# Turning the cross-attention query columns inside the projection, and regrouping the projection's columns

## The chip, the cores and the metric

The kernel runs on one core of a Trainium2 chip, as one program on its five engines: TensorE (PE) multiplies, VectorE (DVE), ScalarE (ACT) and GpSimd (POOL) work on what it leaves in PSUM, and SyncE (SP) starts most of the transfers. The metric is the device time of one execution in microseconds; several executions are timed and their median stands.

## The reference

All tensors are fp32 and there are 256 tokens of width 1024. A first block (pooling mixer, MoBA attention, gated feed-forward) is followed by two layers of a second block. Each of these two layers projects its input, mixes tokens, attends to a memory of 256 rows, projects out, normalises, and runs a mixture of 16 experts. The change touches only how the two input projections are made:

```python
def second_block(x, mem, ...):
    for i in range(DEPTH_2):                       # two layers
        if kind == 0:                              # layer 1: NSA, w_in is 1024 x 2596
            proj = x @ nsa_w_in[j]
            mix = nsa_mixer(proj[..., :-XA_WIDTH], ...)
        elif kind == 1:                            # layer 2: MLA, w_in is 1024 x 672
            proj = x @ mla_w_in[j]
            mix = mla_mixer(proj[..., :-XA_WIDTH], mla_q_norm[j], mla_w_uq[j], ...)
        xq = proj[..., -XA_WIDTH:].reshape(B, S, XA_HEADS, HEAD_DIM_2)   # XA_WIDTH = 256: 4 heads of 64
        xa = memory_cross_attention(xq, mk, mv).reshape(B, S, XA_WIDTH)
        y = jnp.concatenate([mix, xa], -1) @ w_out[i]
        x = layer_norm(DEEPNORM_ALPHA * x + y, ...)
        f = hier_moe(x, ...)                       # 16 experts, each 3 x 1024 x 512
        x = layer_norm(DEEPNORM_ALPHA * x + f, ...)

def mla_mixer(mix_cols, q_norm, w_uq, kv_norm, w_ukv, cos_m, sin_m):
    c_q    = mix_cols[..., :256]                   # the latent vectors
    c_kv   = mix_cols[..., 256:384]
    k_rope = mix_cols[..., 384:416]
    q  = (rms_norm_2(c_q, q_norm) @ w_uq)...       # needs the whole row of c_q
    kv = (rms_norm_2(c_kv, kv_norm) @ w_ukv)...
```

## The kernel before

**The split product.** A large projection is an fp32 product made of three fp32r products (`three`, L796): both operands are split into a rounded high part and the rest, and high x high, high x low, low x high are added in PSUM. The activations lie turned (feature by token) as the pair `h1 = (hTr, yTr)`. Weights come by units of up to 512 columns (`by_cols`, L383) in three slots, and each unit is cut into four pieces of 256 weight rows. For each piece ACT writes the high part `phi` (`cast`, L1960, the copy at L1969) and DVE the low part `plo` (`cut`, L1344, the subtraction at L1349). There are four piece buffers, so a piece is cast when TensorE has used the piece four before it (`s_pc`); hence ACT and DVE cast and cut the *next* unit while TensorE multiplies the present one.

**Two forms of the product.** `tok3` (L818, steps at L805) keeps the activations stationary and moves the weights: two banks, one for each half of the tokens, hold token rows. `feat3` (L821) keeps 128x128 blocks of the weights stationary and moves the 256 tokens: the result comes turned, feature by token. Both record their matmuls at L798. A result in token rows that is wanted turned goes out of PSUM to SBUF and through TensorE's transposes (`turn_cols`, L749, recorded at L755), and out again.

**Layer 1 (the n stage, L992 to L1071).** Columns of `nsa_w_in` come as units n1, n2, n0, then n4 (2048 to 2560), n3 (1536 to 2048) and n5 (2560 to 2596, 36 columns). TensorE interleaves them with the compression of the keys (L1018), the turning of queries, and the compressed scores (`cs`, L1054, 30 columns wide). After n5 (L1057) it turns the window keys (`kw`) and the cross-attention queries (`xq`, L1062), then waits for `s_pcn` and turns the compressed probabilities (`pt`, L1068). `s_pcn` comes from DVE: a softmax over 15 compressed keys, whose first half (L1672 to L1680) goes to ACT for the exponentials (L2158) and whose second half (L1688 to L1700) stands in DVE's program behind `second_row(11, 5, 36, ...)` (L1682), the copy of n5's second result bank. The attention of this layer follows.

**Layer 2 (the m stage, L1258 to L1315).** Columns of `mla_w_in` come as m0 (0 to 512) and m1 (512 to 672, 160 columns), both by `tok3`; `pm` receives the token rows. DVE and ACT copy m1's banks behind the cutting and casting of the next unit's four pieces (ob0, L1873 to L1876 and L2252 to L2255). Only then come the norms' squares (ACT, L2262, four in a row), the variances (DVE, L1879), the inverse roots (POOL, L2307), the scaling (DVE, L1884), and the rotation of `k_rope` (DVE, L1888). TensorE waits for the copies, turns the cross-attention queries (L1266, L755), waits for the scaled latents, turns them (`cq`, `ck`, L1270), and after DVE's copies (L1892, L1895) runs six small projections (L1285, L1288) with the turning of heads between them (L1304). Banks are given in turn of four, so a head's transposes wait for the copy of the ones before (L1333).

**After each attention.** `out_proj`, a layer norm and the router run, then the experts: 96 halves of expert weights of 1 MB each go through 18 places (`expert_loads`, L677). SP issues them in order and waits before each for the event that frees its place: the first ones for the projections' last pieces and for the end of the attention (`s_pv`, 48 and 80), half 18 and on for TensorE's use of the half 18 before. The loads of ob1 and of the next layer's units stand in the same queue.

Of the kernel before, what the change touches and what calls it, by code (L numbers as in the profile page):

```python
# [15 lines left out]
KC = 8  # L16
# [142 lines left out]
def build(nc, ins, out, const, onehot, scratch):  # L159
    ctx = ExitStack()  # L160
    with ctx:
# [221 lines left out]
        def by_cols(name, w, n0, n):  # L383
            unit(name, [cols(w, KC, n0, n)], 2 * n, KC // 2)
# [33 lines left out]
        for c in (4, 3):  # L418
            by_cols(f"n{c}", w_n, c * 512, 512)
        unit("n5", [cols(w_n, KC, 2560, 36)], KC * 36, 1)  # L420
        by_cols("oa0", w_o2[0], 0, 512)
        by_cols("oa1", w_o2[0], 512, 512)
        by_cols("m0", w_m, 0, 512)
        by_cols("m1", w_m, 512, 160)
# [78 lines left out]
        B.work("n", 12, own=False)  # L503
# [17 lines left out]
        B.work("m", 4, own=False)  # L521
        for stage, n in (("xq2", 1), ("cq", 1), ("ck", 1)):
            B.work(stage, n)
# [205 lines left out]
        def tensor_program(e):  # L729
# [301 lines left out]
            tok3_steps(bks, h1, 512, p0, range(3))  # L1031
# [4 lines left out]
            tok3_steps(bks, h1, 512, p0, range(3, 4))  # L1036
# [20 lines left out]
            tok3_steps(two_banks("n", 10), h1, 36, first_piece("n5"), range(1), KC)  # L1057
            e.wait_ge(s_rope, 6)
            turn_cols("kw", pj, 1792 - 64, 5, 64)
            for i in range(10, 12):  # L1060
                e.wait_ge(*B.empty("n", i))
            turn_cols("xq", pj, 2340, 2)  # L1062
# [7 lines left out]
            await_empty("ks", "kw", "xq", "cc1")  # L1070
# [192 lines left out]
            tok3("m", 0, h1, 512, first_piece("m0"))  # L1263
            tok3("m", 2, h1, 160, first_piece("m1"))
            await_empty("m")
            turn_cols("xq2", pm, 416, 2)  # L1266
# [55 lines left out]
        def vector_program(e):  # L1322
# [323 lines left out]
            second_row(7, 4, 512, p0 + 3)  # L1646
# [35 lines left out]
            second_row(11, 5, 36, first_piece("n5"))  # L1682
# [190 lines left out]
            for n, (c0, w) in enumerate(((0, 512), (512, 160))):  # L1873
                p0 = first_piece(f"m{n}")
                cut(p0 + 4, p0 + 8)
                evac("m", 2 * n + 1, pm[:, 1, c0:c0 + w], B.ap("m", 2 * n + 1)[:, 0:w], None, used(p0 + 3, 1))  # L1876
# [18 lines left out]
            evac("ck", 0, ckT[:, 0, :], B.ap("ck", 0)[:, 0:256], colv[:, KN:KN + 1])  # L1895

# [20 lines left out]
            for n in range(6):  # L1917
                project(n)
                if n >= 2:
                    turned_heads(n - 2)  # L1920
# [7 lines left out]
        def scalar_program(e):  # L1928
# [215 lines left out]
            first_row(6, 4, 512, p0 + 3)  # L2144
# [14 lines left out]
            first_row(10, 5, 36, first_piece("n5"))  # L2159
            keys("kw", kwT)  # L2160
            evac("xq", 0, xqT, B.ap("xq", 0)[:, :].rearrange("p (c t) -> p c t", c=2), -0.125)
# [90 lines left out]
            for n, (c0, w) in enumerate(((0, 512), (512, 160))):  # L2252
                p0 = first_piece(f"m{n}")
                cast(p0 + 4, p0 + 8)
                evac("m", 2 * n, pm[:, 0, c0:c0 + w], B.ap("m", 2 * n)[:, 0:w], None, used(p0 + 3, 0))  # L2255
# [7 lines left out]
            evac("xq2", 0, xqT2, B.ap("xq2", 0)[:, :].rearrange("p (c t) -> p c t", c=2), -0.125)  # L2263
# [21 lines left out]
            for n in range(6):  # L2285
                project(n)
                if n >= 2:
                    turned_heads(n - 2)
# [9 lines left out]
        def pool_program(e):  # L2298
# [207 lines left out]
```

## Time and profile before

| | |
|---|---|
| median of 3 executions | 1183.96 us (1181.03 to 1193.82) |
| profiled execution, device time | 1182.21 us |
| its span, first to last instruction | 1180.1 us |
| mean granted TensorE clock (1.00 is 2.4 GHz) | 0.964 |
| PE busy | 1060.3 us, 90% of the span |
| DVE, ACT, POOL busy | 39%, 32%, 10% |
| HBM read | 294.58 MB, 251 GB/s over the span |

Every instruction has a start and a duration; a busy share says only that records cover the time. The steps between the starts of consecutive matmuls, not their own durations, give their price, since they overlap. The chain of waits is followed back from the last instruction and names what each step waited for.

### The profile page before, as it was taken

To read this page: it belongs to the slowest core of one execution; us is meant where nothing else is said; L and a number is where in the kernel's file an instruction comes from. 1 tells how busy PE (TensorE), PEld (TensorE's weight loads), DVE (VectorE), ACT (ScalarE), POOL (GpSimd) and SP (SyncE) were. 2 spreads that over 40 slices of the span, in tenths; PEclk is the share of its full clock that TensorE was granted. 3 is DMA by queue.
4 is the path that set the end of the run, shared out by engine and by line. 5 is a ranking of instruction groups with operands and counts; after the bars stand their busy time and mean duration, and the time that the engine had idled before them with its cause. 6 is when DMAs were issued, how large, how long until landed. Compare 5 with 4: busy or idle time off the path is not lost.

```text
span 1180.1 us, 15606 instructions
## 1 busy us (share of the span) xinstructions
PE 1060.3 (90%) x6167; PEld 730.3 (62%) x6167; DVE 457.6 (39%) x975; ACT 373.3 (32%) x726; POOL 121.8 (10%) x151
## 2 busy tenths in 40 slices
PE   5999999999998998997999999857888799999983
PEld 5967899998867787674644444326557464445431
DVE  4644566665466445654111111035555311111103
ACT  4443355554355454731111111114462111111101
POOL 0711011110001001420000000010042000000001
PEclk9999999999999998998899999988899889999998
DMA  9834665554454441079899999983319789999993
GB/s 338 189 142 137 218 208 174 185 192 165 159 198 145 141 175 46 2 282 346 325 387 386 386 387 387 387 312 110 126 46 337 278 326 387 386 386 387 387 388 124
DMA packets 164577, 296.95 MB, mean 252 GB/s; under 512 B 10975, under 2 KB 40847, under 8 KB 164495
## 3 DMA queue, kind: packets, MB, share of 16 engines
q1 hardware_dynamic: 162910, 290.08, 69.1%
q0 software_dynamic: 1584, 5.77, 1.3%
q8 instruction: 53, 0.87, 0.3%
q14 instruction: 30, 0.24, 0.1%
HBM read 294.58 MB, written 1.25 MB: 251 GB/s over the span
## 4 chain that ended last, share of the span: by engine, by line
PE 75%; DMA 8%; DVE 7%; ACT 5%; issue 3%; POOL 1%; POOLq 1%; DVEq 0%; SPq 0%; ACTq 0%
PE ps L798 32%; PE ps L1135 16%; PE ps L1149 6%; PE ps L1121 6%; DMA arena<-in_moe_w_down 3%; DMA arena<-in_moe_w_up 2%; DMA gain_rows<-in_moe_w_up 2%; PE ps L1162 2%; PE ps L900 2%; PE ps L869 1%; PE ps L879 1%; PE ps L792 1%; ACT ring L1998 1%; PE ps L1285 1%; POOL small L2307 1%
## 5 line engine op out<-in xcount | busy, mean ns | idle before, releaser
L1349 DVE TENSOR_TENSOR plo<-w,phi 128x1024 fp32r<-128x1024 f32 (+1 forms) x143 | 174.5, 1233 | 163.0 <-ACT phi L1969 162.5
L1969 ACT CAST phi<-w 128x1024 fp32r<-128x1024 f32 (+1 forms) x143 | 144.9, 1029 | 169.5 <-PE ps L798 161.1
L1135 PE MATMUL ps<-w,arena 128*64 128x512 f32 x528 | 135.7, 594 | 3.5 <-DMA w<-in_moe_w_up 3.5
L798 PE MATMUL ps<-hTr,phi 128*128 128x256 f32 x448 | 128.5, 287 | 4.5 <-DVE yTr L1339 4.5
L798 PE MATMUL ps<-hTr,plo 128*128 128x256 f32 x448 | 128.1, 286 | 0.0
L798 PE MATMUL ps<-yTr,phi 128*128 128x256 f32 x448 | 128.0, 286 | 0.0
L1829 DVE SCALAR_TENSOR_TENSOR yTr<-ps,small,yTr 128x512 fp32r<-128x512 f32 x32 | 24.0, 751 | 237.5 <-ACT yTr L2208 237.5
L798 PE MATMUL ps<-phi,hTr 128*128 128x512 f32 (+2 forms) x272 | 103.8, 382 | 6.3 <-DVE yTr L1339 6.3
L798 PE MATMUL ps<-phi,yTr 128*128 128x512 f32 (+2 forms) x272 | 103.5, 381 | 3.4 <-issue 1.9
L1149 PE MATMUL ps<-w,ring 128*64 128x512 f32 x336 | 92.4, 593 | 6.6 <-DMA w<-in_moe_w_down 3.6
L798 PEld LDWEIGHTS ps<-hTr,phi 128*128 128x128 f32 x448 | 87.4, 195 | 5.1 <-issue 3.1
L798 PEld LDWEIGHTS ps<-yTr,phi 128*128 128x128 f32 x448 | 87.4, 195 | 0.0
L798 PEld LDWEIGHTS ps<-hTr,plo 128*128 128x128 f32 x448 | 87.2, 195 | 0.0
L1135 PEld LDWEIGHTS ps<-w,arena 128*64 128x64 f32 x528 | 42.0, 137 | 72.7 <-issue 72.5
L1135 PE MATMUL ps<-arena 128*64 128x512 f32 x304 | 79.1, 594 | 4.4 <-DMA arena<-in_moe_w_up 4.4
L1121 PEld LDWEIGHTS ps<-mkT,x 128*128 128x128 f32 x512 | 67.8, 217 | 13.7 <-issue 9.7
L1121 PE MATMUL ps<-mkT,x 128*128 128x128 f32 x512 | 70.7, 304 | 3.7 <-DVE mkT L1805 3.7
L798 PE MATMUL ps<-plo,hTr 128*128 128x512 f32 (+2 forms) x176 | 65.9, 374 | 0.0
L1149 PEld LDWEIGHTS ps<-w,ring 128*64 128x64 f32 x336 | 29.4, 137 | 56.0 <-issue 56.0
L798 PEld LDWEIGHTS ps<-phi,hTr 128*128 128x128 f32 x272 | 52.6, 193 | 16.4 <-issue 7.1
L798 PEld LDWEIGHTS ps<-phi,yTr 128*128 128x128 f32 x272 | 52.7, 194 | 13.6 <-issue 4.2
L1135 PEld LDWEIGHTS ps<-arena 128*64 128x64 f32 x304 | 24.9, 137 | 52.6 <-issue 52.6
(299 smaller groups left out, 1559.3 us busy)
## 6 DMA issues: line engine op xcount, KB each, us to landing
w<-in_moe_w_down SPq DMA_DIRECT2D x42, 1024.0 KB, 14.3
w<-in_moe_w_gate SPq DMA_DIRECT2D x38, 1024.0 KB, 14.0
w<-in_moe_w_up SPq DMA_DIRECT2D x28, 1024.0 KB, 14.2
arena<-in_moe_w_up SPq DMA_DIRECT2D x24, 1024.0 KB, 14.2
w<-in_w_up SPq DMA_DIRECT2D x22, 1024.0 KB, 7.6
arena<-in_moe_w_down SPq DMA_DIRECT2D x16, 1024.0 KB, 14.3
arena<-in_moe_w_gate SPq DMA_DIRECT2D x14, 1024.0 KB, 14.2
w<-in_w_out SPq DMA_DIRECT2D x6, 2048.0 KB, 8.2
```

What stands on the lines that cost most here:

```text
L792: ins_ = e.matmul(B.ap("kv0", i)[:, q * 256:q * 256 + 256], l, r, start=(k == 0), stop=(k == KC - 1))
L798: ins_ = e.matmul(o, l[a], r[b], start=first and i == 0, stop=last and i == 2, skip_group_check=group)
L869: ins_ = e.matmul(psum[2 * (u % 2) + j["half"]][:, q * 256:q * 256 + w], lq, kk, start=True, stop=True)
L879: ins_ = e.transpose(bk[:, o * 128:o * 128 + 128], prob(j["J"])[:, c:c + 128], ident)
L900: ins_ = e.matmul(ob[hp:hp + 64, t * 128:t * 128 + 128], *m[o], start=(o == 0), stop=(o == len(m) - 1))
L1121: ins_ = e.matmul(psum[2 + hf][:, c * 128:c * 128 + 128], x[:, t, kc * 128:kc * 128 + 128], one_hots[p % 2][:, t, :], start=(t == 0), stop ...
L1135: ins_ = e.matmul(bank[64 * ee:64 * ee + 64, :], xgs[p % 2][:, o:o + 64], half_view(kind, p, ee, ab)[:, c, :], start=(k == 0), stop=(k == 7))
L1149: ins_ = e.matmul(psum[2 + hf][64 * ee:64 * ee + 64, :], Pb[p % 2][:, o:o + 64], half_view("d", p, ee, hf)[:, f, :], start=(f == 0), stop= ...
L1162: ins_ = e.matmul(psum[4 + 2 * t + hf][:, :], bts[p][:, t * 128:t * 128 + 128], y_parts[part][:, hf * 512:hf * 512 + 512], start=(p == 0 a ...
L1349: e.tensor_tensor(plo[:, 0:m], slots[u % 3][:, j * m:j * m + m], phi[:, 0:m].bitcast(F32), ALU.subtract).then_inc(s_cut)
L1829: e.scalar_tensor_tensor(y_parts[1][:, part], psum[2 + hf][:, :], slot_gate[:, p:p + 1], y_parts[0][:, part].bitcast(F32), ALU.mult, ALU.s ...
L1969: e.copy(pieces[p % 4][0][:, 0:m], slots[u % 3][:, j * m:j * m + m]).then_inc(s_cast)
```

## The change

In layer 1 the last unit holds the second 128 cross-attention query columns and is multiplied with the weights stationary, straight into the turned form; n4 shrinks to 420 columns. In layer 2 m0 shrinks to the 416 latent columns, and m1 is all 256 query columns, with the weights stationary. The copy of m0 and the norms' chain come right behind m0; two pairs of ob0's pieces are cast and cut later, among the small projections. POOL waits for m1's last use before it writes rotated keys, since they lie over `hTr`.

```diff
@@ units
-        for c in (4, 3):
-            by_cols(f"n{c}", w_n, c * 512, 512)
-        unit("n5", [cols(w_n, KC, 2560, 36)], KC * 36, 1)
+        by_cols("n4", w_n, 2048, 420)
+        by_cols("n3", w_n, 1536, 512)
+        unit("n5", [cols(w_n, KC, 2468, 128)], KC * 128, 1)
...
-        by_cols("m0", w_m, 0, 512)
-        by_cols("m1", w_m, 512, 160)
+        by_cols("m0", w_m, 0, 416)
+        by_cols("m1", w_m, 416, 256)
@@ TensorE, layer 1
-            tok3_steps(two_banks("n", 10), h1, 36, first_piece("n5"), range(1), KC)
+            bk, pc = claim("xh", 0), cut(first_piece("n5"))
+            for c in range(KC):
+                ins_ = three(bk[:, 0:256], [a[:, c * 128:c * 128 + 128] for a in pc], [a[:, c, :] for a in h1], c == 0,
+                             c == KC - 1)
+            ins_.then_inc(s_pc, 2)
...
-            turn_cols("xq", pj, 2340, 2)
+            turn_cols("xq", pj, 2340, 1)
@@ TensorE, layer 2
-            tok3("m", 0, h1, 512, first_piece("m0"))
-            tok3("m", 2, h1, 160, first_piece("m1"))
+            tok3("m", 0, h1, 416, first_piece("m0"))
+            bk, p0 = claim("xq2", 0), first_piece("m1")
+            for j in range(4):
+                pc = cut(p0 + j)
+                for c in range(2):
+                    for q in range(2):
+                        o = q * 256 + c * 128
+                        ins_ = three(bk[:, c * 256:c * 256 + 256], [a[:, o:o + 128] for a in pc],
+                                     [a[:, 2 * j + q, :] for a in h1], ...)
+                ins_.then_inc(s_pc, 2)
             await_empty("m")
-            turn_cols("xq2", pm, 416, 2)
@@ DVE, layer 1
-            second_row(11, 5, 36, first_piece("n5"))
@@ DVE, layer 2
-            for n, (c0, w) in enumerate(((0, 512), (512, 160))):
-                p0 = first_piece(f"m{n}")
-                cut(p0 + 4, p0 + 8)
-                evac("m", 2 * n + 1, pm[:, 1, c0:c0 + w], B.ap("m", 2 * n + 1)[:, 0:w], None, used(p0 + 3, 1))
+            cut(p0 + 4, p0 + 7)
+            evac("m", 1, pm[:, 1, 0:416], B.ap("m", 1)[:, 0:416], None, used(p0 + 3, 1))
+            cut(p0 + 7, p0 + 8)
...
             evac("ck", 0, ckT[:, 0, :], B.ap("ck", 0)[:, 0:256], colv[:, KN:KN + 1])
+            p0 = first_piece("ob0")
+            cut(p0, p0 + 2)
...
                 project(n)
+                if n == 1:
+                    cut(p0 + 2, p0 + 4)
                 if n >= 2:
                     turned_heads(n - 2)
@@ ACT, layer 1
-            first_row(10, 5, 36, first_piece("n5"))
+            evac("xh", 0, xqT[:, 1, :], B.ap("xh", 0)[:, 0:256], -0.125, used(first_piece("n5"), 1))
             keys("kw", kwT)
-            evac("xq", 0, xqT, B.ap("xq", 0)[:, :].rearrange("p (c t) -> p c t", c=2), -0.125)
+            evac("xq", 0, xqT[:, 0, :], B.ap("xq", 0)[:, 0:256], -0.125)
@@ ACT, layer 2: as on DVE, with cast for cut; the queries' copy stays behind the squares
+            cast(p0 + 4, p0 + 7)
+            evac("m", 0, pm[:, 0, 0:416], B.ap("m", 0)[:, 0:416], None, used(p0 + 3, 0))
+            cast(p0 + 7, p0 + 8)
...
+            p0 = first_piece("ob0")
+            cast(p0, p0 + 2)
...
+                if n == 1:
+                    cast(p0 + 2, p0 + 4)
@@ POOL, layer 2
             e.wait_ge(s_mrope, 2)
+            e.wait_ge(*used(first_piece("m1") + 3, 1))
```

## Rows read from the trace of the kernel before

**Rows 1.** The page: what the transfers moved, in 40 equal slices of the span.

```profile
GB/s 338 189 142 137 218 208 174 185 192 165 159 198 145 141 175 46 2 282 346 325 387 386 386 387 387 387 312 110 126 46 337 278 326 387 386 386 387 387 388 124
```

**Rows 2.** Chain of waits, experts of layer 1: start, length, what it was.

```profile
719.33 14.29 DMA arena<-in_moe_w_up
```

**Rows 3.** Stretches: busy time per engine, granted clock, DMA share, GB/s.

```profile
446.00:500.00 54.00, 48.07 (x426) 36.42 (x427) 32.81 (x161) 35.01 (x134) 19.67 (x14) 0.91 0.01 2
860.00:878.00 18.00, 16.05 (x121) 10.27 (x120) 10.95 (x56) 12.17 (x50) 7.64 (x9) 1.00 0.01 2
```

**Rows 4.** Chain of waits, layer 1 from unit n4 to the compressed probabilities.

```profile
408.09 8.19 PE ps L798 x36
...
441.42 2.60 PE ps L1054 x24
444.02 8.52 PE ps L798 x48
...
456.55 2.81 PE ps L1068 x24
```

**Rows 5.** DVE in order of time, round n5; brackets: idle before, and releaser.

```profile
445.55 0.35 DVE L1680 TENSOR_TENSOR arena<-arena,small 128x180 f32<-128x180 f32 x1
452.56 0.20 DVE L1331 COPY arena<-ps 128x36 f32<-128x36 f32 x1 [6.67 <-PE ps L798]
452.67 0.34 DVE L1688 TENSOR_TENSOR arena<-arena,cst 128x180 f32<-128x180 f32 x1
```

**Rows 6.** ACT in order of time: the second half of the exponentials.

```profile
445.92 0.35 ACT L2158 ACTIVATE arena<-arena 128x180 f32<-128x180 f32 x1 [0.66 <-DVE arena L1680]
```

**Rows 7.** Stretches as in rows 3, round n5.

```profile
444.00:445.00 1.00, 1.00 (x12) 1.00 (x11) 0.93 (x4) 0.09 (x1) 0.00 (x0) 1.00 1.04 383
446.00:448.00 2.00, 2.00 (x11) 2.00 (x11) 0.00 (x0) 0.46 (x2) 0.00 (x0) 0.50 0.02 7
```

**Rows 8.** Chain of waits, layer 2 from m0 to the third small projection.

```profile
802.28 16.48 PE ps L798 x96
818.78 1.05 ACT phi L1969
819.86 1.23 DVE plo L1349
...
821.43 0.52 ACT ring L2262 x2
...
825.31 1.01 DVE arena L1884 x4
...
829.27 5.46 PE ps L1285 x8
...
836.59 2.60 PE ps L1285 x8
```

**Rows 9.** Stretches as in rows 3, after TensorE stops at 818.8.

```profile
820.00:821.00 1.00, 0.00 (x0) 0.00 (x0) 1.00 (x1) 0.02 (x1) 0.00 (x0) 1.00 0.00 0
824.00:826.00 2.00, 0.00 (x0) 0.00 (x0) 0.69 (x3) 0.00 (x0) 1.11 (x2) 0.50 1.01 391
```

**Rows 10.** Chain of waits, a long run of 256-column matmuls of L798.

```profile
140.94 128.44 PE ps L798 x1056
```

**Rows 11.** TensorE in order of time, 160-column matmuls: second and second last.

```profile
813.33 0.28 PE L798 MATMUL ps<-plo,hTr 128*128 128x160 f32 x1
...
818.36 0.27 PE L798 MATMUL ps<-plo,hTr 128*128 128x160 f32 x1
```

**Rows 12.** DVE, layer 2: the copies of 512 columns, and the third projection's copy.

```profile
814.36 0.68 DVE L1331 COPY arena<-ps 128x512 f32<-128x512 f32 x1
...
839.28 0.56 DVE L1331 COPY hT<-ps 128x384 f32<-128x384 f32 x1 [1.96 <-PE ps L1285]
```

**Rows 13.** ACT in order of time: casts of two pieces back to back.

```profile
800.98 2.00 ACT L1969 CAST phi<-w 128x1024 fp32r<-128x1024 f32 x2
```

**Rows 14.** Stretches as in rows 3: the attention of layer 1.

```profile
460.00:503.00 43.00, 38.02 (x384) 26.50 (x382) 29.23 (x153) 32.80 (x132) 20.71 (x15) 1.00 0.01 2
```

More of the change, by code:

```diff
@@ L502, in build @@
         B.work("x3", 4)
-        B.work("n", 12, own=False)
+        B.work("n", 10, own=False)
+        B.work("xh", 1, own=False)
         for stage, n in (("kc", 6), ("ks", 3), ("ch0", 1), ("ch1", 1), ("qt", 3), ("cc0", 1), ("cc1", 1), ("kt", 1), ("cs", 2),
@@ L520, in build @@
         B.work("x4", 4)
-        B.work("m", 4, own=False)
-        for stage, n in (("xq2", 1), ("cq", 1), ("ck", 1)):
+        B.work("m", 2, own=False)
+        B.work("xq2", 1, own=False)
+        for stage, n in (("cq", 1), ("ck", 1)):
             B.work(stage, n)
@@ L1030, in tensor_program @@
             bks, p0 = two_banks("n", 6), first_piece("n4")
-            tok3_steps(bks, h1, 512, p0, range(3))
+            tok3_steps(bks, h1, 420, p0, range(3))
             e.wait_ge(*loaded("cmp"))
@@ L1035, in tensor_program @@
             hidden(0)
-            tok3_steps(bks, h1, 512, p0, range(3, 4))
+            tok3_steps(bks, h1, 420, p0, range(3, 4))
             hidden(1)
@@ L1056, in tensor_program @@
                 ins_.then_inc(B.sem_full("cs", t))
-            tok3_steps(two_banks("n", 10), h1, 36, first_piece("n5"), range(1), KC)
+            bk, pc = claim("xh", 0), cut(first_piece("n5"))
[3 more added lines that the diff above has]
+            ins_.then_inc(s_pc, 2)
             e.wait_ge(s_rope, 6)
             turn_cols("kw", pj, 1792 - 64, 5, 64)
-            for i in range(10, 12):
+            for i in range(6, 8):
                 e.wait_ge(*B.empty("n", i))
-            turn_cols("xq", pj, 2340, 2)
+            turn_cols("xq", pj, 2340, 1)
             e.wait_ge(s_pcn, 2)
@@ L1069, in tensor_program @@
                 ins_.then_inc(B.sem_full("pt", c))
-            await_empty("ks", "kw", "xq", "cc1")
+            await_empty("ks", "kw", "xq", "xh", "cc1")
             attention(1)
@@ L1262, in tensor_program @@
             await_empty("x4")
-            tok3("m", 0, h1, 512, first_piece("m0"))
-            tok3("m", 2, h1, 160, first_piece("m1"))
+            tok3("m", 0, h1, 416, first_piece("m0"))
[6 more added lines that the diff above has]
+                        ins_ = three(bk[:, c * 256:c * 256 + 256], [a[:, o:o + 128] for a in pc],
+                                     [a[:, 2 * j + q, :] for a in h1], j == 0 and q == 0 and c == 0,
+                                     j == 3 and q == 1 and c == 1, True)
+                ins_.then_inc(s_pc, 2)
             await_empty("m")
-            turn_cols("xq2", pm, 416, 2)
             bk = claim("cq", 0)
@@ L1645, in vector_program @@
             cut(p0 + 5, p0 + 8)
-            second_row(7, 4, 512, p0 + 3)
+            second_row(7, 4, 420, p0 + 3)
             evac("qt", 1, qT2[:, 2:4, :], B.ap("qt", 1)[:, :].rearrange("p (c t) -> p c t", c=2), -0.125)
@@ L2143, in scalar_program @@
             cast(p0 + 7, p0 + 8)
-            first_row(6, 4, 512, p0 + 3)
+            first_row(6, 4, 420, p0 + 3)
             hidden(1)
@@ L2251, in scalar_program @@
             cast(p0 + 2, p0 + 4)
[L2252 to L2255, printed above, removed]
+            cast(p0 + 4, p0 + 7)
+            evac("m", 0, pm[:, 0, 0:416], B.ap("m", 0)[:, 0:416], None, used(p0 + 3, 0))
+            cast(p0 + 7, p0 + 8)
             for sem_, n in B.all_empty("m"):
@@ L2262, in scalar_program @@
                     e.activation(Lb[0][:, 0:w], pm[:, t, c0:c0 + w], ACT.Square, accum_out=sqm[:, n, t:t + 1]).then_inc(s_msq)
-            evac("xq2", 0, xqT2, B.ap("xq2", 0)[:, :].rearrange("p (c t) -> p c t", c=2), -0.125)
+            evac("xq2", 0, xqT2, B.ap("xq2", 0)[:, :].rearrange("p (c t) -> p c t", c=2), -0.125,
+                 used(first_piece("m1") + 3, 1))
+            p0 = first_piece("ob0")
+            cast(p0, p0 + 2)
             def project(n):
```

## The prediction

> **What bounds the kernel now.** I read four views in this order: the page, the chain of waits, the stretches of time, and single engines in order of time round the two places that the diff touches.
>
> On the page look for where the transfers run at their ceiling: 386 to 388 GB/s over both expert stages, and 46 and 2 GB/s ahead of the first [rows 1]. In the chain, TensorE stops in the experts of layer 1 and a weight transfer of 14.29 us takes its place [rows 2], and layer 2 does the same. So the end of each expert stage is set by 96 MB of weights, and time saved inside it would be worth little. Time saved ahead of it is another matter. Its transfers cannot start early: between 446 and 500 us, and between 860 and 878, the core moves 2 GB/s [rows 3], since SP waits for the attention and for the output projection's pieces. Their places in SBUF come free with that work, and half 18 and on are released by TensorE's own use. Whatever ends the attention earlier moves the whole expert stage with it, one for one. The question is then only: by how much do the two attentions start earlier?
>
> In layer 1 the chain is TensorE without a gap from unit n4 to the end of n5 (452.5 us), and then DVE's softmax until 456.55, where the compressed probabilities are turned [rows 4]. Two things are to be seen. n5 is 48 matmuls of only 36 columns and takes 8.52 us. And DVE stands idle for 6.67 us ahead of n5's copy although the exponentials were long there: the rest of the softmax is queued behind that copy [rows 5, 6]. In the same stretch the granted clock falls from 1.00 to 0.50, that is from 2.4 to 1.2 GHz, with TensorE recorded busy all the time, on 30- and 36-column matmuls [rows 7].
>
> In layer 2 the chain is m0 and m1 on TensorE (16.48 us), one cast, one cut, a copy, the norms on ACT, DVE, POOL and DVE, and the first small projection at 829.27 [rows 8]. TensorE waits or does odd transposes for 10.5 us, and its clock goes from 1.00 to 0.50 [rows 9]; so the first projection takes 5.46 us, the third, of the same shape, 2.60 [rows 8].
>
> **Prices.** A 512-column matmul steps by 8.19/36 = 0.2275 us [rows 4], a 256-column one by 128.44/1056 = 0.1216 us [rows 10]. From 813.33 to 818.36 lie 45 steps of 160 columns, 0.112 us each [rows 11]. Between 256 and 512 the slope is 0.000414 us a column, so 420 columns cost 0.1895 and 416 cost 0.1878. No row has the three new shapes' neighbours nearer; the bounds for them are 0.1216 and 0.2275.
>
> **Layer 1.**
> 1. n4: 48 matmuls go from 512 to 420 columns, 48 x (0.2275 - 0.1895) = 1.8 us less; all on the path.
> 2. n5: 48 narrow ones become 24 of 256 columns, 24 x 0.1216 = 2.9 us at full clock. The row of before is 8.52.
> 3. DVE's copy of n5's bank is gone, so the second half of the softmax no longer waits for n5 at all. It can start at 445.9, the end of the first half, in place of 452.67 [rows 5]; the exponentials it needs are in by 446.3 [rows 6]. It gives 6.7 us. Its own length, 456.5 - 452.7 = 3.8 us, stays.
> 4. Is TensorE ready by then? On the old clock, less step 1, the scores end at 442.2, n5 at 445.1, and 12 transposes in place of 14 end by 446.5. DVE releases the probabilities at 456.5 - 6.7 - 1.8 = 448.0. So n5's new price is hidden by 1.5 us; at half clock, 24 x 0.213 = 5.1 us and slower transposes, it would be late by about 2.
> 5. ACT copies a turned bank of 256 columns instead of 36, and half of `xq`: less in sum, and in the time that it idled. The larger load of n5 (512 KB for 144) stands in SP's queue ahead of the loads of oa0 and oa1. ACT's cast of oa0 would come about 1 us later; behind it DVE has a copy that TensorE's n3 releases only later. Nothing if it stays under 1.5 us, otherwise the excess.
>
> Layer 1: 1.8 + 6.7 = **8.5 us** earlier (bounds: 6.5 with the clock low, 9.5).
>
> **Layer 2.**
> 1. m0: 48 x (0.2275 - 0.1878) = 1.9 less; m1: 48 x (0.1216 - 0.112) = 0.5 more. m0 ends at 802.3 + 9.0 = 811.3, m1 at 818.8 - 1.4 = 817.4.
> 2. m0's copy no longer stands behind ob0's pieces. DVE's takes at most 0.68 us [rows 12], so `pm` is complete at 811.9. From the first square to the last scaling took 821.43 to 826.32, 4.9 us [rows 8]; now that ends at 816.9, beside m1, half a microsecond ahead of m1's end. In between DVE has only one narrower cut.
> 3. From the end of the scaling to the first projection were 829.27 - 826.32 = 2.95 us (latents turned, `k_rope` rotated, two copies). Counted from 816.9 it gives 819.9, from m1's end 820.3. I take 820.1: **9.2 us** earlier. The transposes of the queries and their wait are gone; they lay in TensorE's idle time.
> 4. The clock. TensorE would now idle for less than 2 us at a time. Before, it stopped at 818.8 and the clock was still 1.00 two microseconds later [rows 9]. So the first projection should take 2.60: **2.9 us** more. If it falls all the same, 0.
> 5. ob0's pieces, before hidden under m1's matmuls, now lie in the projections. The first two fit: DVE is free from 819.9 to the end of the first projection at 822.7 and needs 2 x 1.2 us. The second two stand behind the second projection. There DVE had idled for 1.96 us before the copy of the third [rows 12]; now it waits for ACT's first cast (1.0) and cuts twice (1.23 each, rows 8), 3.4 us. So the copy and all behind it, the head rotations and the copy that frees a bank for TensorE's transposes, come 3.4 - 2.0 = **1.4 us** late, once. ACT's two casts, 2.00 us [rows 13], end before that. Bounds: 0 and 3.4.
> 6. POOL's new wait ends with m1, at 817.4; it needs the rotated `k_rope` at 818.4 anyway. Queued behind it are only its six copies. ob1's load is queued on SP behind ob0's last cut, some 8 us later; it is wanted only after the attention, and SP's next item, an expert half, comes behind the fifth projection.
>
> Layer 2: 9.2 + 2.9 - 1.4 = **10.7 us** earlier (bounds 6 and 12).
>
> A rule can be set against the slope. The Trainium skill, "TensorE: Matmul & The Clock Gate", sections "Back-to-back issue gap" and "LDWEIGHTS (loading the stationary operand)", makes a matmul cost its columns at 2.4 GHz plus 2.5 ns, and a load of 128 stationary columns 107 ns. By it n4 saves 48 x 38 ns = 1.8 us, and m0 with m1 48 x 37.5 ns = 1.8 in place of my 1.4. The sum would be 0.4 us better.
>
> **Sum.** 8.5 + 10.7 = 19.2 us. The profiled execution took 1182.2 us of device time (span 1180.1 and 2.1 around it), so 1163.0, with a span near 1161. The median shown for before, 1183.96, lies 1.8 above its profiled execution; 1163.0 is 1.8% under that median. About 1% is what a measurement of this kernel can tell from no change.
>
> **Rivals.**
> *A, the clock falls anyway* (0.17). In layer 1 it fell while TensorE was busy, so small matmuls are no safeguard, and the 30-column scores remain [rows 4, 7]. For: fewer narrow matmuls does not mean none. Against: wide ones follow after 2.6 us. Layer 1 then loses 2.0, layer 2 the 2.9 of step 4: 1165 to 1168. The Trainium skill, "TensorE: Matmul & The Clock Gate", Part 1, says that an idle array is throttled and sustained work frees it; here the trace is stricter, since its records show no idleness before the fall in layer 1.
> *B, layer 1's gain is swallowed by the expert weights* (0.06). If some transfer kept the end of the first expert stage where it is, only layer 2 counts: 1182.2 - 10.7 = 1171.5. The 2 GB/s ahead of both stages speak against it [rows 3].
> *C, the chain does not lie beside m1* (0.08), because ACT's or DVE's copy is held by m0's last piece. Then m1's end comes first and 4.9 us of chain follow it, and the clock falls again: layer 2 gives 1.4 and what the copy's place saves (2.6), less 1.4: 1171.
> *D, slower* (0.04). Attention in layer 1 runs with TensorE at full clock [rows 14]. If it were entered at 1.2 GHz, with nothing but small matmuls to bring the clock back, and stayed there, the 38 us that TensorE is busy in it would near 76, at up to 38 us in all: 1182.2 - 19.2 + 38 = 1201. It decides from 19.2 us of extra busy time, that is with half of the attention at the low clock. Against it: the clock of that stretch is 1.00 although n5, shortly before it, ran at 0.50 [rows 7].
> *E, no measurable change* for causes that I have not named: 0.05.
>
> **How the numbers follow.** My forecast has 0.60, A 0.17, B 0.06, C 0.08, D 0.04, E 0.05. The likeliest case's own bounds are 1182.2 less 21.5, and less 16.5: 1160.7 to 1165.7. With A, B and C, and 3 us either way should the clock fall or rise elsewhere at another moment (the 2.9 of step 4), the range is 1158 to 1172, which leaves out D, E and a part of the rest. Faster by over 1% means under 1172.1: the forecast, A, and nearly all of B and C, 0.86 by the cases; since B and C sit at the bound I say 0.84, 0.12 within 1%, 0.04 slower.
>
> **What would show it.** n5 as 24 matmuls in about 3 us at clock 1.00. DVE without an idle time over 1 us between the halves of the softmax, and the probabilities turned some 5.8 us after the scores end, in place of 12.5. The squares starting within 1 us of m0's end; the first projection 2.5 to 3 us after m1's end, and 2.6 us long; an idle time on TensorE before a head's transposes that is 1.4 us longer. The stretch of 2 GB/s before each expert stage as long as before. I am wrong if the attentions start 19 us earlier in sum and the end does not, or if the projections' gap holds a wait for `plo`.

## The result, and the profile after

| | before | after |
|---|---|---|
| median | 1186.32 us (1181.03 to 1193.82, 4 runs) | 1168.76 us (1164.50 to 1169.89, 4 runs) |
| ratio after/before | | 0.9833 [0.9801, 0.9866] |
| profiled execution, its span | 1182.21, 1180.1 us | 1164.50, 1162.0 us |
| mean granted clock | 0.964 | 0.970 |

By the ratio the change makes the kernel 1.7% faster (interval 1.3 to 2.0%); the difference is 17.6 us by the medians, 17.7 by the profiled executions. Forecast were 19.2. The median of 1168.8 lies in the range, 5.8 us above the 1163.0 named and 3.1 above the likeliest case's own bounds. 4.3 of the 5.8 is that after's median lies above its own profiled execution, the fastest of its four; before's median lies above its own too (by 4.1 us here, 1.8 in the three runs shown first). The stretches of the traces, and not this one total, show what the change did.

The page of after, what the transfers moved, in 40 slices:

```profile
GB/s 337 197 145 134 222 216 172 192 179 184 136 227 145 132 116 121 2 300 344 326 386 386 387 386 387 387 351 68 218 29 371 252 348 387 387 387 386 387 388 118
```

It is the picture of [rows 1]: 2 GB/s ahead of the first expert stage, 386 to 388 in both. The chain of waits after, the experts of layer 1, still has the weight transfer of [rows 2] (start, length, what):

```profile
710.18 14.26 DMA arena<-in_moe_w_up
```

**Layer 1.** Chain of waits after, answering to [rows 4] (L798 has become L800, L1054 L1056 and L1068 L1074):

```profile
407.83 6.89 PE ps L800 x36
...
433.72 5.69 PE ps L800 x24
...
447.50 2.81 PE ps L1074 x24
```

TensorE in order of time, the scores (24 matmuls), n5 from its first to its last matmul, the queries' transposes and those of the probabilities (brackets: idle before, and releaser):

```profile
439.24 2.76 PE L1056 MATMUL ps<-small,arena 128*128 128x30 f32 x24
441.83 0.37 PE L800 MATMUL ps<-hTr,phi 128*128 128x256 f32 x1
...
444.67 0.28 PE L800 MATMUL ps<-hTr,plo 128*128 128x256 f32 x1
444.79 1.47 PE L757 MATMUL ps<-cst,arena 128*128 128x128 f32 x12
447.50 2.68 PE L1074 MATMUL ps<-cst,arena 128*15 128x128 f32 x23 [1.24 <-DVE arena L1713]
```

DVE where its idle 6.67 us were [rows 5], and the stretch after, whose clock was 0.50 before [rows 7] (columns: length; busy time of TensorE, its weight loads, DVE, ACT, POOL; granted clock; DMA share; GB/s):

```profile
443.52 0.35 DVE L1694 TENSOR_TENSOR arena<-arena,small 128x180 f32<-128x180 f32 x1
443.79 0.34 DVE L1701 TENSOR_TENSOR arena<-arena,cst 128x180 f32<-128x180 f32 x1
```

```profile
445.00:446.00 1.00, 1.00 (x12) 1.00 (x10) 0.86 (x3) 0.95 (x3) 0.00 (x0) 1.00 0.06 12
```

n5 lasts 2.96 us, DVE goes from one half of the softmax to the other without a pause, and TensorE now waits 1.24 us for DVE ahead of the probabilities, which it turns 5.5 us after the scores end (447.50 less 442.00), in place of 12.5. The chain of waits now runs over DVE from its copy of n3's bank (439.43) to the end of the softmax, and n5 is no longer on it.

**Layer 2.** Chain of waits after, from m0 to the attention's first scores, answering to [rows 8]:

```profile
792.88 9.34 PE ps L800 x48
802.24 0.62 ACT phi L1985
802.92 0.52 ACT ring L2277 x2
...
804.88 0.25 DVE small L1891 x2
...
806.81 1.01 DVE arena L1896 x4
...
810.77 4.36 PE ps L1299 x8
815.14 1.88 PE ps L1302 x4
...
817.69 0.95 ACT phi L1985
818.73 0.92 DVE plo L1363
819.88 1.22 DVE plo L1363
821.09 0.47 DVE hT L1345
...
834.21 1.56 PE ps L871 x8
```

TensorE in order of time, the end of m1, the transposes of the latents, the first projection and the first head's transposes:

```profile
807.66 0.28 PE L800 MATMUL ps<-hTr,plo 128*128 128x256 f32 x1
807.96 0.63 PE L1284 MATMUL ps<-cst,arena 128*128 128x128 f32 x4
808.43 0.38 PE L1288 MATMUL ps<-cst,arena 128*128 128x128 f32 x2
810.77 4.36 PE L1299 MATMUL ps<-w,arena 128*128 128x384 f32 x8 [1.96 <-DVE arena L1347]
...
824.33 0.64 PE L1318 MATMUL ps<-cst,arena 128*96 128x128 f32 x4 [1.16 <-DVE arena L1347]
```

The norm's chain runs from 802.92 to 807.8, beside m1, which ends at 807.96. Then come 2.8 us of transposes and copies, 1.96 of them without TensorE, and the first projection: 4.36 us and not 2.60. Its clock, in the stretches after:

```profile
809.00:810.00 1.00, 0.00 (x0) 0.00 (x0) 0.96 (x4) 1.00 (x2) 0.48 (x2) 1.00 0.00 0
...
811.00:812.00 1.00, 1.00 (x4) 0.60 (x4) 1.00 (x2) 0.00 (x0) 0.81 (x1) 0.94 0.00 0
...
813.00:814.00 1.00, 1.00 (x3) 0.67 (x2) 0.00 (x0) 0.09 (x1) 0.00 (x0) 0.50 0.00 0
```

TensorE waited from 808.8 to 810.77. The clock was still 1.00 in the wait, and fell about a microsecond after it (0.94 over the second microsecond of the rows above), with the projection under way.

**Where the span's 18.1 us came from**, cut at the same instructions in both traces (times in us, before to after):

| from, to | before | after | difference |
|---|---|---|---|
| start of the span to n4's first matmul | 408.09 | 407.83 | -0.3 |
| n4's first matmul to the probabilities turned | 48.46 | 39.67 | -8.8 |
| to m0's first matmul (unchanged code) | 345.73 | 345.38 | -0.35 |
| m0's first matmul to the attention's | 50.17 | 41.33 | -8.8 |
| to the end (unchanged code) | 327.65 | 327.79 | +0.1 |

Both gains stand in the stretches that the diff touches, and what follows passes them on one for one. The first line hides two unchanged stretches that went opposite ways: the units n1, n2 and n0 began 2.9 us earlier (365.8 in place of 368.6), and from there to n4 it took 2.6 longer; their first matmuls ran at clock 0.50 in this execution.

### The profile page after: what moved, and what is told of

It is laid out like the page before. It is cut to its first block, busy times and chain, and to the rows that moved or that the text cites. A ratio compares the mean times of both kernels' runs of the same rounds, so it can differ in the third digit from the quotient of the medians.

```text
span 1162.0 us, 15542 instructions
## 1 busy us (share of the span) xinstructions
PE 1047.2 (90%) x6137; PEld 720.3 (62%) x6137; DVE 457.0 (39%) x973; ACT 372.6 (32%) x725; POOL 122.8 (11%) x151
## 4 chain that ended last, share of the span: by engine, by line
PE 74%; DMA 8%; DVE 7%; ACT 5%; issue 3%; POOL 1%; POOLq 1%; DVEq 0%; SPq 0%; ACTq 0%
PE ps L800 32%; PE ps L1141 17%; PE ps L1155 7%; PE ps L1127 6%; DMA arena<-in_moe_w_down 3%; DMA gain_rows<-in_moe_w_up 2%; DMA arena<-in_moe_w_up 2%; PE ps L1168 2%; PE ps L902 2%; PE ps L871 1%; PE ps L881 1%; PE ps L794 1%; ACT ring L2014 1%; ACT gain_rows L2014 1%; POOL small L2327 1%
## 5 line engine op out<-in xcount | busy, mean ns | idle before, releaser
L1363 DVE TENSOR_TENSOR plo<-w,phi 128x1024 fp32r<-128x1024 f32 (+3 forms) x143 | 174.6, 1235 | 160.6 <-ACT phi L1985 160.4
L1985 ACT CAST phi<-w 128x1024 fp32r<-128x1024 f32 (+3 forms) x143 | 144.6, 1028 | 164.8 <-PE ps L800 156.4
L800 PE MATMUL ps<-hTr,phi 128*128 128x256 f32 x472 | 134.7, 285 | 4.6 <-DVE yTr L1353 4.6
L800 PE MATMUL ps<-hTr,plo 128*128 128x256 f32 x472 | 134.2, 284 | 0.0
L800 PE MATMUL ps<-yTr,phi 128*128 128x256 f32 x472 | 134.2, 284 | 0.0
L800 PE MATMUL ps<-phi,hTr 128*128 128x512 f32 (+2 forms) x240 | 94.2, 392 | 6.2 <-DVE yTr L1353 6.2
L800 PE MATMUL ps<-phi,yTr 128*128 128x512 f32 (+2 forms) x240 | 93.5, 389 | 3.4 <-issue 1.9
L800 PEld LDWEIGHTS ps<-hTr,phi 128*128 128x128 f32 x472 | 91.3, 193 | 5.1 <-issue 3.1
L800 PEld LDWEIGHTS ps<-yTr,phi 128*128 128x128 f32 x472 | 91.4, 194 | 0.0
L800 PEld LDWEIGHTS ps<-hTr,plo 128*128 128x128 f32 x472 | 91.3, 193 | 0.0
L800 PE MATMUL ps<-plo,hTr 128*128 128x512 f32 (+2 forms) x144 | 55.9, 388 | 0.0
L800 PEld LDWEIGHTS ps<-phi,hTr 128*128 128x128 f32 x240 | 45.7, 191 | 15.5 <-issue 7.0
L1857 DVE TENSOR_TENSOR ring<-ring,ps 128x512 f32<-128x512 f32 x16 | 11.0, 688 | 111.1 <-PE ps L1141 111.1
```

Source lines behind the costliest of these rows:

```text
L800: ins_ = e.matmul(o, l[a], r[b], start=first and i == 0, stop=last and i == 2, skip_group_check=group)
L1363: e.tensor_tensor(plo[:, 0:m], slots[u % 3][:, j * m:j * m + m], phi[:, 0:m].bitcast(F32), ALU.subtract).then_inc(s_cut)
L1985: e.copy(pieces[p % 4][0][:, 0:m], slots[u % 3][:, j * m:j * m + m]).then_inc(s_cast)
```

## The experiments

Two stretches are measured in every run's trace. *Stretch 1* runs from n4's first matmul record to the probabilities turned: 48.7 us before, 39.9 after (the chain's 48.46 and 39.67 begin 0.25 later). *Stretch 2* runs from m0's first matmul to the attention's: 50.2 and 41.3. They repeat within 0.2 us where nothing in them changes and the clock does what it did, while whole executions of one kernel differ by several microseconds. The theory before these runs: the two halves of the change act alone and add up; layer 1's comes from DVE's softmax that no longer stands behind n5, layer 2's from the norm beside m1, and what is missing is the clock of the first projection.

### Each half alone

`n_only` keeps layer 1's half of the change and has layer 2 as before, `m_only` the reverse; both are shown here against the changed kernel:

```diff
 n_only
-        by_cols("m0", w_m, 0, 416)
-        by_cols("m1", w_m, 416, 256)
+        by_cols("m0", w_m, 0, 512)
+        by_cols("m1", w_m, 512, 160)
...
+            turn_cols("xq2", pm, 416, 2)
 m_only
-        by_cols("n4", w_n, 2048, 420)
...
-        unit("n5", [cols(w_n, KC, 2468, 128)], KC * 128, 1)
+        unit("n5", [cols(w_n, KC, 2560, 36)], KC * 36, 1)
...
+            second_row(11, 5, 36, first_piece("n5"))
```

> The change of layer 1 alone (n4 narrower, n5 wide and turned, DVE's copy of n5 gone); layer 2 as before. Theory (two independent gains, each passed on whole through the expert stage): the stretch from n4's first matmul to the turning of the compressed probabilities takes 39.7 us as in the changed kernel, against 48.5 before; m0's first matmul to the first matmul of the attention stays 50.2; the time falls by 8.5 to 9 us, ratio 0.9925. Rival (the expert weights' transfers hold the end of the first expert stage): same 39.7, but no more than 2 us less in all.

> The change of layer 2 alone (m0 of 416 columns, m1 turned, norms beside m1, ob0's pieces among the small projections); layer 1 as before. Theory: 48.5 us in layer 1's stretch, 41.3 in layer 2's (50.2 before), time lower by 9, ratio 0.9925; with layer 1 alone the two sum to the whole change. Rival (the two gains are not independent, since the place of the clock's falls moves with layer 1's end): layer 2's stretch differs from 41.3 by over 1 us.

| | median us | ratio to before | stretch 1 | stretch 2 |
|---|---|---|---|---|
| before | 1186.21 | 1 | 48.7 | 50.2 |
| n_only | 1176.70 | 0.9914 [0.9869, 0.9960] | 40.1 | 50.1 |
| m_only | 1176.41 | 0.9914 [0.9870, 0.9957] | 48.8 | 41.5 |

Each half gives its stretch what it has in the whole change, and 9.5 and 9.8 us of time by the medians, with intervals of some 5 us either way. Layer 1's half alone makes the kernel faster by more than its rival's 2 us (0.9960 at most), so its gain is not swallowed by the expert weights behind it.

### Order or width: what layer 1 gained from

`n_order` is the kernel before with DVE's copy of n5 behind the softmax. It removes DVE's wait and leaves n5 at 48 matmuls of 36 columns:

```diff
                 e.tensor_tensor(p3, p3, cms[:, 0, :].unsqueeze(2).broadcast_to([128, 12, NCMP]),
                                 ALU.subtract).then_inc(s_csx)
-            second_row(11, 5, 36, first_piece("n5"))
             for t in range(2):
...
                 e.tensor_tensor(p3, p3, cms[:, 3, :].unsqueeze(2).broadcast_to([128, 12, NCMP]), ALU.mult).then_inc(s_pcn)
+            second_row(11, 5, 36, first_piece("n5"))
```

`n_wait` is the opposite: the changed kernel, wide n5, with the wait put back.

```diff
+            e.wait_ge(*used(first_piece("n5"), 1))
             for t in range(2):
```

> The kernel before with one line moved: DVE copies n5's bank after the second half of the softmax instead of ahead of it; n5 stays 48 matmuls of 36 columns. If the copy's place in DVE's program were the cause of the 6.7 us, the compressed probabilities would be turned near 450 us instead of 456.5. My theory now: TensorE itself is not free earlier, since n5 ends at 452.5 and 14 transposes at the low clock take it to 455.8, so the stretch of layer 1 falls by under 1 us (48.5 to about 47.8) and the time by no more than can be measured.

> The changed kernel with DVE's wait put back: the second half of the softmax waits for the end of n5's matmuls, now 24 of 256 columns. If the wait itself were the cost, layer 1's stretch would return to near 48.5. My theory: n5 now ends 1.0 us after DVE's first half, so the stretch takes 40.8 against 39.7.

*n_order*: median 1189.71, ratio 1.0013 [0.9969, 1.0056]; stretch 1 is 47.75, only 1.0 less. DVE in order of time, and TensorE:

```profile
448.64 0.35 DVE L1699 TENSOR_TENSOR arena<-arena,small 128x180 f32<-128x180 f32 x1
452.26 0.20 DVE L1331 COPY arena<-ps 128x36 f32<-128x36 f32 x1 [3.27 <-PE ps L798]
```

```profile
452.06 3.25 PE L755 MATMUL ps<-cst,arena 128*128 128x128 f32 x14
455.10 1.16 PE L1068 MATMUL ps<-cst,arena 128*15 128x128 f32 x8
```

The softmax ends at 449.0, some 7 us earlier. TensorE is still in n5 until 452.1, at half clock, and turns the probabilities only at 455.1. The idle DVE was a symptom: behind it stood the slow n5 itself.

What made n5 slow can be read from its steps. TensorE in order of time, n5's 36-column matmuls in the kernel before (the second, the 18th, the 20th and the last), then 256-column ones in after_again, the changed kernel run once more, in which the clock fell to 0.50 within n5:

```profile
443.97 0.26 PE L798 MATMUL ps<-plo,hTr 128*128 128x36 f32 x1
...
445.75 0.36 PE L798 MATMUL ps<-phi,yTr 128*128 128x36 f32 x1
...
446.17 0.38 PE L798 MATMUL ps<-plo,hTr 128*128 128x36 f32 x1
...
452.14 0.38 PE L798 MATMUL ps<-phi,yTr 128*128 128x36 f32 x1
```

```profile
443.19 0.41 PE L800 MATMUL ps<-hTr,phi 128*128 128x256 f32 x1
...
445.53 0.41 PE L800 MATMUL ps<-hTr,plo 128*128 128x256 f32 x1
```

At full clock a 36-column matmul steps by 1.78/16 = 0.111 us, at half clock by 5.97/28 = 0.213. A 256-column one steps by 0.120 in after at full clock (22 steps from its second, at 442.03, to its last, at 444.67), and by 2.34/11 = 0.213 here at half clock. So the narrow ones were hardly cheaper, and n5 gained by being 24 matmuls in place of 48. At full clock the 48 would take 48 x 0.111 = 5.3 us (an estimate), against 2.96; the other 3.2 of the 8.5 was the low clock.

*n_wait*: one execution, 1169.11 us; stretch 1 is 42.8 where 40.8 was expected. Of the 2.9 us over the changed kernel, half is not the edit's: n4's first 36 matmuls, ahead of it, took 8.28 us in place of 6.89, and the clock in their first part was 0.50:

```profile
408.00:410.00 2.00, 2.00 (x7) 1.89 (x7) 0.00 (x0) 0.00 (x0) 0.00 (x0) 0.50 0.00 0
```

The wait itself shows on DVE, and from the scores' end to the probabilities it cost 6.88 - 5.51 = 1.4 us:

```profile
446.16 0.35 DVE L1702 TENSOR_TENSOR arena<-arena,cst 128x180 f32<-128x180 f32 x1 [1.12 <-PE ps L800]
```

So, of layer 1's 8.8: the order alone 1.0; the columns alone (39.9 + 1.4 = 41.3) 7.4; both 8.8. Nearly all of it is n5 as 24 matmuls, and n4's narrowing (1.7: 1.3 in its first 36, 0.4 in the other 12). The 1.4 comes from one execution of n_wait.

### The norm not beside m1

`m_late_norm` holds ACT's squares back until m1 has ended, and changes nothing else:

```diff
             for sem_, n in B.all_empty("m"):
                 e.wait_ge(sem_, n)
+            e.wait_ge(*used(first_piece("m1") + 3, 1))
```

> The changed kernel with one wait added: ACT's squares wait for m1's last matmul, so the norms' chain follows m1 as it did before the change; the queries still come turned and the copy of m0 still stands behind m0. Theory (most of layer 2's gain is the chain lying beside m1): the squares start at m1's end, 5.0 us later than in the changed kernel, and the first small projection comes 5 us later; with the low clock from its start, up to 1 us on top: stretch of layer 2 46.3 to 47.5 us against 41.3, time 5 to 6 us above the changed kernel. Rival (the gain came from the transposes and copies that are gone, and the chain is short enough anyway): under 2 us.

Median 1177.43 against 1189.00, ratio 0.9893 [0.9866, 0.9921]; stretch 2 is 48.1. ACT and TensorE in order of time:

```profile
817.83 0.42 ACT L2278 ACTIVATE ring<-arena 128x256 f32<-128x256 f32 x1 [5.21 <-PE ps L800]
```

```profile
822.86 1.09 PE L1284 MATMUL ps<-cst,arena 128*128 128x128 f32 x4 [5.14 <-DVE arena L1896]
...
825.66 4.35 PE L1299 MATMUL ps<-w,arena 128*128 128x384 f32 x8 [1.29 <-DVE arena L1347]
```

It is 6.8 us longer than in the changed kernel, all ahead of the first projection. Of it 1.8 is m0 itself, which began this execution at clock 0.50 (stretch below), before any edited instruction; m0 and m1 took 16.90 us in place of 15.1. The other 5.0 is the chain of the norm, put behind m1: what its place beside m1 is worth. The copy's new place, without the overlap, is seen in the same trace: the projection comes 8.0 us after m1, where before it was 10.5. By the ratios (0.9893 against 0.9833) the edit takes back some 7 us of the change's 20; their intervals leave room for some 2 to 12, so they can't tell 5.0 from 6.8. The 5.0 is what the trace ties to the edit.

```profile
802.00:804.00 2.00, 2.00 (x7) 1.94 (x6) 1.31 (x2) 0.00 (x0) 0.00 (x0) 0.50 0.00 0
```

### The two residues of layer 2: ob0's cuts and the clock

`spread` parts ob0's last two pieces, one behind each of two projections:

```diff
-                if n == 1:
-                    cut(p0 + 2, p0 + 4)
+                if n in (1, 3):
+                    cut(p0 + 2 + n // 2, p0 + 3 + n // 2)
...
-                if n == 1:
-                    cast(p0 + 2, p0 + 4)
+                if n < 2:
+                    cast(p0 + 2 + n, p0 + 3 + n)
```

`warm` puts six idle matmuls of 384 columns into TensorE's wait; the bank is overwritten by the first projection.

```diff
+            bk = claim("mp0", 0)
+            for _ in range(6):
+                e.matmul(bk[:, 0:384], wq_[:, 0, 0:128], wq_[:, 0, 0:384], start=True, stop=True)
             await_empty("cq", "ck")
```

`both` has the two edits together.

> The changed kernel with the second two pieces of ob0 placed one at a time: ACT casts one behind each of the first two projections, DVE cuts one behind the second and one behind the fourth, each into an idle time of some 2 us. Theory (the two cuts in a row delay the third projection's copy by 1.4 us): TensorE's wait of 1.16 us ahead of the head transposes and its 0.30 before go back to 0.41 in all, stretch of layer 2 40.1 us instead of 41.3. Rival (the delay is the copies' own, and spreading moves it to the later projections): 41.3 as before.

> The changed kernel with six matmuls of 384 columns added whose result is overwritten, between the turning of the latents and the first small projection, so that TensorE does not idle there. Theory (the clock falls during the first projection because of the 2 us in which TensorE waited just before): the first projection takes 2.6 us instead of 4.4 and layer 2's stretch 39.6 to 40.2 instead of 41.3. Rival (the fall comes from the transposes and the end of the wide matmuls, whatever fills the wait): 4.4 us, and the stretch as before or longer by what the added matmuls take beyond the wait.

> The last two together, spread cuts and added matmuls. If both theories hold: stretch of layer 2 near 38.5 us instead of 41.3, time 2 to 3 us under the changed kernel. If the clock's part falls: 40.1.

| | median us | ratio to before | stretch 2 | first projection |
|---|---|---|---|---|
| spread | 1166.67 | 0.9816 [0.9793, 0.9838] | 39.9 | 4.51 |
| warm | 1168.70 | 0.9830 [0.9803, 0.9856] | 41.7 | 2.74 |
| both | 1163.35 | 0.9795 [0.9773, 0.9816] | 40.2 | 2.74 |

*spread*: the third projection's copy is now held for 0.49 us only, and TensorE's wait before the first head's transposes is 0.33 us in place of 1.16. Stretch 2 loses 1.4 us, as expected.

```profile
821.50 1.23 DVE L1363 TENSOR_TENSOR plo<-w,phi 128x1024 fp32r<-128x1024 f32 x1
823.21 0.56 DVE L1345 COPY hT<-ps 128x384 f32<-128x384 f32 x1 [0.49 <-PE ps L1299]
```

*warm*: the clock stays at 1.00 and the projection takes 2.74 us. So its 4.36 was the clock. But the fill overran its place: 4.11 us, where the wait was 1.96, since each such matmul is two records (chain of waits):

```profile
811.96 4.11 PE ps L1325 x12
816.07 2.58 PE ps L1299 x8
```

The stretch is no shorter. I had priced six fills within the wait; cause right, price wrong. The price stood in a row of before: the third projection, four matmuls of this shape, is 8 records and 2.60 us [rows 8], 0.65 each. *both* missed its expected 38.5 for the same reason. Its median is nonetheless the lowest, and its profiled execution does not say why: stretch 1, which it does not touch, was 41.4 there, 1.5 us longer than elsewhere.

### A shorter fill, and a shorter wait

`both3` is `both` with three fills in place of six. `rope_spread` is `spread` and, in place of a fill, shortens the wait: half of `k_rope`'s rotation goes behind the copies that the projection waits for. `rope_spread_fill` adds two fills to that. `after_again` is the changed kernel once more, beside them.

```diff
 rope_spread
             tr = [a[:, 0:16] for a in tmp4]
-            for t in range(2):
-                rope(pm[:, t, 384:400], pm[:, t, 400:416], t, 8, 24, [], tr).then_inc(s_mrope)
-                e.wait_ge(s_mrope, t + 1)
+            rope(pm[:, 0, 384:400], pm[:, 0, 400:416], 0, 8, 24, [], tr).then_inc(s_mrope)
...
             evac("ck", 0, ckT[:, 0, :], B.ap("ck", 0)[:, 0:256], colv[:, KN:KN + 1])
+            e.wait_ge(s_mrope, 1)
+            rope(pm[:, 1, 384:400], pm[:, 1, 400:416], 1, 8, 24, [], tr).then_inc(s_mrope)
```

> Spread cuts, and three added matmuls of 384 columns in place of six: six came out as twelve records and 3.9 us where the wait is 2.0. Theory: three fill 1.95 us, the clock stays at 1.00 through the first projection (2.6 us), and layer 2's stretch is 38.2 to 38.5 against 40.2 with six and 39.9 with none. Rival (the longer fill was needed to hold the clock): first projection near 4.4, stretch 40.

> Spread cuts; and DVE rotates k_rope's second half of tokens only after it has copied the turned latents, 0.75 us that TensorE no longer waits for. Theory: the first projection starts 0.5 to 0.7 us earlier than 3.1 us behind m1's last matmul; if the wait of 1.4 us is short enough for the clock to stay up, it also takes 2.6 instead of 4.4: stretch 37.5 to 37.7; if the clock falls as before, 39.3. POOL's copies of the rotated keys come later and are hidden by the projections.

> As the one before, with two added matmuls of 384 columns (four records, 1.3 us) in the wait. Theory: clock at 1.00, first projection 2.6 us, stretch of layer 2 37.6 to 38.0 against 41.3 in the changed kernel; time 3 to 4 us under it. Rival: what is saved ahead of the attention comes back in it; then the stretch is short and the time is not.

> The changed kernel itself once more, on the chip and in the rounds of the three that follow, for a direct comparison. Theory: stretches of 39.7 (layer 1) and 41.3 us (layer 2) again; the profiled stretch ahead of layer 1 differs by a few us from run to run, since it does so between runs that share its code.

| | median us | ratio to before | stretch 2 | first projection |
|---|---|---|---|---|
| both3 | 1167.25 | 0.9821 [0.9798, 0.9844] | 38.3 | 2.74 |
| rope_spread | 1165.65 | 0.9813 [0.9782, 0.9844] | 37.6 | 2.82 |
| rope_spread_fill | 1163.64 | 0.9796 [0.9771, 0.9821] | 37.7 | 2.74 |
| after_again | 1167.02 | 0.9828 [0.9798, 0.9859] | 41.4 | 4.51 |

In rope_spread TensorE waits 1.34 us, with nothing put into the wait, and the clock stays up:

```profile
812.93 2.82 PE L1299 MATMUL ps<-w,arena 128*128 128x384 f32 x8 [1.34 <-DVE arena L1347]
```

```profile
814.00:815.00 1.00, 1.00 (x5) 0.60 (x4) 1.00 (x2) 0.51 (x2) 0.85 (x2) 1.00 0.00 0
```

The stretch that the change brought from 50.2 to 41.3 can be brought to 37.6. What this is worth in time is less clear. The three kernels are 1.8 to 2.0% faster than before, but their intervals overlap with that of after_again. The medians lie 3.4 us below it (rope_spread_fill), 1.4 below it (rope_spread), and 0.2 above (both3). That they beat the changed kernel is not shown.

The reason is in unchanged code, and the traces name the place. From the probabilities turned to m0's first matmul after took 345.4 us, after_again 347.8, and others up to 351.4; nearly all of the difference lies in the attention of layer 1. Chain of waits, the same pieces of it in after and in after_again, whose clock was 0.50 there:

```profile
459.84 0.95 PE ps L902 x12
460.79 1.09 PE ps L871 x8
```

```profile
460.76 1.67 PE ps L902 x12
462.43 2.01 PE ps L871 x8
```

From the probabilities turned to the output projection's first matmul it is 50.8 us in the six traces whose clock stays at 1.00 there (before, m_only, after, both, both3, rope_spread_fill). It is 53.4 where the clock is 0.50 for some 7 us of it (after_again, n_only, n_wait, spread, warm, rope_spread), 55.0 in m_late_norm and 56.2 in n_order. It differs between executions of one kernel, after and after_again. Whether the change makes it more frequent, no run here tells: 7 of the 11 traces with the new layer 1 have it, and 1 of the 3 with the old.

## Why the prediction was right, and where not

**What bounds the kernel.** Held. From the second attention's first matmul to the end nothing changed but 0.1 us, and the 2 GB/s stretch before the experts is there. Rival B falls with n_only.

**Layer 1, steps 1 to 5** (8.5 forecast, 8.8 measured). n4's 36 first matmuls step by 6.89/36 = 0.191 us (0.1895 forecast), n5 lasts 2.96 us (2.9 forecast), and it is hidden by 1.24 us (1.5). The load of n5 delayed nothing: ACT's cast of oa0 waits 3.06 us for its transfer, before 3.03. In this execution the clock did not fall in n5, but that was not sure: it did in after_again, n_only and warm, 3 of the 11 traces with the new layer 1. n5 then takes 4.5 us, and stretch 1 only 0.15 us more (40.06 for 39.91), since DVE's softmax still comes later. Step 4 had put "late by about 2" on that case, and rival A 2.0: A's condition is met in some executions, its price in layer 1 was far too high. The mechanism of step 3, though, was half told. "It gives 6.7 us" credits the order on DVE, and n_order shows that the order alone gives 1.0. Step 4, TensorE ready in time, was the condition; I used it as a check, and it is the larger part of the gain. With the narrow n5 it fails by 6 us. The sum came out because both were changed together.

**Layer 2, steps 1 to 3** (9.2 forecast, 9.1 measured). m0 and m1 take 15.1 us where 16.48 stood, 1.4 less as worked out, and not the 1.8 of the rule set against the slope. The squares start 0.7 us after m0's last matmul ends (802.20), their chain ends beside m1, and the projection comes 2.8 us after m1. Rival C is what m_late_norm builds: the missing overlap costs 5.0 us there, close to the 4.9 put on it.

**Step 4, the clock: the term that was mis-sized.** It read 2.9 us and was 5.46 - 4.36 = 1.1. The step argued from [rows 9], clock still 1.00 two microseconds after TensorE's stop, that idle times under 2 us are harmless. TensorE did idle for only 1.96 us, and the clock did fall, after the wait was over. It did so in all five traces with this wait (after, after_again, m_only, n_wait, spread), so it was no chance of one execution. That rows show 1.00 two microseconds into an idle time does not say that the fall will not come; it came late before, too. In layer 2 rival A, with 0.17, was the true case, but it charged the whole 2.9 and the fall cost 1.8. Not all of the 2.9 was to be had, either: behind a wait and at clock 1.00 the projection takes 2.82 (rope_spread), and not the 2.60 of one that follows other work. So the likeliest case, as it was written, did not come about; the forecast is near because this term was one of several. The Trainium skill, "TensorE: Matmul & The Clock Gate", Part 1, ties the clock to whether the array works; warm, which fills the wait, and rope_spread, which shortens it, agree (1.00 in both), as do both, both3 and rope_spread_fill.

**Step 5, ob0's pieces** (1.4 forecast). From the first projection's end to the attention the time grew by 1.35 us, and spread takes 1.4 of stretch 2 away. TensorE's waits in it grew by 1.05 (1.16 and 0.30 us, where 0.41 stood); "1.4 us longer" for the one wait before a head's transposes was too much. **Step 6** held: no wait of POOL's on m1 stands in the chain.

**The sum.** 8.8 + 9.1 + 1.1 - 1.35 = 17.6 where 8.5 + 9.2 + 2.9 - 1.4 = 19.2 stood. The 1.6 missing are the clock term (-1.8), with 0.2 from elsewhere. The likeliest case's lower gain, 16.5 us, is worked out nowhere in the prediction. The 1163.0 took before's profiled execution as its base; from the median of 1186.3 the same 19.2 us lead to 1167.1, 1.7 us from what was measured. Rivals D and E are out: the kernel is faster, beyond its interval. D's low clock in the attention of layer 1 did come in other executions, and cost 2.7 to 5.5 us and not 38.

## What to carry to other kernels

An engine that idles ahead of one instruction points at a queue order, but price both: the order, and the producer it waits for; here moving the instruction gave 1.0 us and regrouping the columns 7.4. Count matmuls before columns: 48 of 36 columns took longer than 24 of 256. A chain of small dependent steps is best started beside a matmul stage, and regrouping the columns so that its inputs come first is a cheap way to do it (5.0 us here). When a forecast counts on the clock staying up across a short wait, read the stretches after that wait too.

## What the runs showed of the hardware

- A wait of 1.96 us on TensorE was followed by a fall from clock 1.00 to 0.50, about a microsecond after work had resumed, in after, after_again, m_only, n_wait and spread: 4.36 to 4.51 us for the first projection. A wait of 1.34 us in the same place (rope_spread, one trace) was not followed by one: 2.82 us. Where between them, or on what else, it turns, no run here tells.
- A matmul of 36 columns steps by 0.111 us at full clock and 0.213 at half (before), one of 256 columns by 0.120 (after) and 0.213 (after_again).
- The clock can fall with TensorE recorded busy: in before within n5 (1.00 to 0.50 near 445.8), in after_again at 442.5, both behind 24 matmuls of 30 columns. In after it did not.
- A plain f32 matmul of 384 columns shows as two records and costs 4.11/6 = 0.69 us at full clock (warm), against 0.19 for one matmul of 416 columns of the split operands.
- In unchanged code the clock falls in some executions and not in others. n4 or m0 began at 0.50 in n_wait, both, m_late_norm and n_order and cost 1.4 to 1.8 us; the attention of layer 1 took 50.8, 53.4, 55.0 or 56.2 us. Steps like these are larger than the effects that the last experiments looked for, and only the stretches could show those.
